# PEER decoder kernel: VectorE makes the low part of every second expert weight tile instead of every fourth

## The reference

```
h = rmsnorm(x) * (1 + sc1) + sh1;   x = x + g1 * mixer(h)      # RG-LRU heads and gated DeltaNet heads
h = rmsnorm(x) * (1 + sc2) + sh2;   x = x + g2 * peer(h)
y = rmsnorm(x)

peer: q = h @ peer_wq; scores of 8 heads x 2 halves against 128 keys; top 16 of each half,
      top 16 of their sums -> 16 experts idx (of 16384) and softmax gates for each head
      act = gelu(sum_d u[idx, d] * h[d]);  out = sum_k gates_k * act_k * v[idx_k]
```

## Time and profile before

| | us |
|---|---|
| median of 3 executions | 4352.23 (4347.91 to 4360.71) |
| the profiled execution | 4374.36 |
| its span in the trace | 4372.5 |
| TensorE matmul busy | 3735.8 (85%) |
| VectorE busy | 3022.4 (69%) |
| GpSimd busy | 2100.9 (48%) |
| ScalarE busy | 1476.1 (34%) |
| DMA moved | 1090.19 MB, mean 249 GB/s |

### The profile page before, as it was taken

One profiled execution on the slowest core, in us unless ns is written; L12 is line 12 of the kernel. 1 busy time (PEld: TensorE's weight loads), 2 busy tenths in 40 slices (PEclk: granted clock), 3 DMA queues, 4 the chain that ended last, 5 costly groups with the idle time before them and its releaser, 6 DMA issues. The chain is left out here.

```text
span 4372.5 us, 65820 instructions
## 1 busy us (share of the span) xinstructions
PE 3735.8 (85%) x24298; PEld 3475.5 (79%) x24298; DVE 3022.4 (69%) x4531; ACT 1476.1 (34%) x1889; POOL 2100.9 (48%) x1164
## 2 busy tenths in 40 slices
PE   6876999998896898987669999999988888888887
PEld 3336888988886797987569898889988888888886
DVE  5777645455545223898967777777878888888886
ACT  5665343434442113222323333333332222222222
POOL 2433222222224233324346777677766767666662
PEclk9997999999997998998889999999999999999898
DMA  8981222222222123223369999999999999999994
GB/s 308 355 319 51 83 79 83 73 79 71 68 69 97 54 96 110 82 71 106 144 269 389 414 406 405 393 402 409 399 376 378 394 387 402 388 400 399 408 403 154
DMA packets 253104, 1090.19 MB, mean 249 GB/s; under 512 B 25353, under 2 KB 78857, under 8 KB 172297
## 3 DMA queue, kind: packets, MB, share of 16 engines
q1 hardware_dynamic: 167440, 543.60, 33.8%
q0 software_dynamic: 73728, 536.90, 30.1%
q10 hardware_dynamic: 11776, 7.52, 0.6%
HBM read 1047.54 MB, written 40.40 MB: 249 GB/s over the span
## 5 line engine op out<-in xcount | busy, mean ns | idle before, releaser
L248 POOL TENSOR_TENSOR wlo<-raw,whi 128x1024 fp32r<-128x1024 f32 x551 | 1342.5, 2440 | 1470.8 <-ACT whi L244 1465.4
L244 ACT CAST whi<-raw 128x1024 fp32r<-128x1024 f32 x670 | 697.0, 1049 | 1242.0 <-DMA raw<-in_u 541.0
L263 PE MATMUL gps<-hi_d,whi 128*128 128x320 f32 x2048 | 663.1, 324 | 161.5 <-POOL wlo L248 108.0
L2110 PE MATMUL gps<-chi,whi 128*128 128x320 f32 x2048 | 651.1, 318 | 101.6 <-DVE outacc L2239 85.0
L263 PE MATMUL gps<-lo_d,whi 128*128 128x320 f32 x2048 | 653.6, 319 | 0.0
L263 PE MATMUL gps<-hi_d,wlo 128*128 128x320 f32 x2048 | 652.8, 319 | 0.0
L2110 PE MATMUL gps<-clo,whi 128*128 128x320 f32 x2048 | 640.7, 313 | 0.0
L2110 PE MATMUL gps<-chi,wlo 128*128 128x320 f32 x2048 | 640.6, 313 | 0.0
L2197 DVE SCALAR_TENSOR_TENSOR dps<-ring,coef,dps 128x2048 f32<-128x2048 f32 x252 | 591.6, 2348 | 6.3 <-DMA ring<-in_v_rows,spi 1.6
L2184 DVE CUSTOM_DVE_ANT_0 ring<-ring,dps 128x2048 f32<-128x2048 f32 x256 | 581.9, 2278 | 0.0
L263 PEld LDWEIGHTS gps<-hi_d,whi 128*128 128x128 f32 x2048 | 404.0, 197 | 179.0 <-POOL wlo L248 118.1
(11 more groups left out here) (388 smaller groups left out, 6026.6 us busy)
## 6 DMA issues: line engine op xcount, KB each, us to landing
raw<-in_u SPq DMA_DIRECT2D x256, 512.0 KB, 10.6
raw<-in_v SPq DMA_DIRECT2D x256, 512.0 KB, 7.8
wada<-in_w_ada SPq DMA_DIRECT2D x96, 1024.0 KB, 6.5
raw<-in_w_in SPq DMA_DIRECT2D x96, 512.0 KB, 3.5
gateD<-gst SPq DMA_DIRECT2D x8, 2560.0 KB, 7.5
gate<-gateD SPq DMA_DIRECT2D x32, 640.0 KB, 17.3
raw<-in_w_out SPq DMA_DIRECT2D x32, 512.0 KB, 3.6
raw<-in_w_q SPq DMA_DIRECT2D x32, 512.0 KB, 4.0
```

The costliest lines, as they stand in the source:

```text
L244: act.copy(whi[:, k.slot, :], raw_of(k)).then_inc(W.hi, 1)
L248: pool.tensor_tensor(wlo[:, k.slot, :], raw_of(k), whi[:, k.slot, :].bitcast(F32), ALU.subtract).then_inc(W.lo, 1)
L263: m = pe.matmul(gps[:, bank, 0:DT], w, x[:, kt, :], start=(kt == 0 and n == 0), stop=(kt == KT - 1 and n == 2))
L2110: m = pe.matmul(gps[:, 2 + dt, 0:DT], w[:, slot, cols], x[:, buf, c, :], start=(c == 0 and n == 0), stop=(c == NG - 1 and n == 2))
```

## The change

`by_dve` now picks the slots 1 and 3 from tile 181 on and no longer slot 3 alone from 183 on: VectorE makes tiles j = 1, 3, 5, 7 of each piece, GpSimd j = 0, 2, 4, 6. The counts in `lo_done` follow (two low parts of each engine in four tiles), and one more empty instruction raises the start value of VectorE's semaphore. The instructions themselves, the buffers and the order of each engine's list are the same; 124 low parts leave GpSimd's list and stand in VectorE's (123 before, 247 after), in A behind `clo` of step c, in B between the two additions of a step.

```diff
         def by_dve(k):
 
-            return k.c >= N_SHARED - 1 and k.slot == 3
+            return k.c >= N_SHARED - 3 and k.slot % 2 == 1 and not (isinstance(k.n, int) and k.n < N_SHARED)
 
         def lo_done(k):
 
             m = k.c - N_SHARED
             if by_dve(k):
-                return W.lo_dve, m // 4 + 2 + k.i * (k.per // 4)
+                return W.lo_dve, m // 2 + 3 + k.i * (k.per // 2)
             if m < -4 or m < 0 and isinstance(k.n, int):
                 return W.lo, k.n + 1
-            return W.lo, N_SHARED + m // 4 * 3 + m % 4 + 1 + k.i * (k.per // 4 * 3)
+            return W.lo, N_SHARED + m // 2 + 1 + k.i * (k.per // 2)
...
-                    dve.engine_nop().then_inc(W.lo_dve, 1)
+                    for n in range(2):
+                        dve.engine_nop().then_inc(W.lo_dve, 1)
```

## The result

The changed kernel takes 4480.33 us (median of 4, 4477.44 to 4483.45) against 4355.02 us before: a ratio of 1.0274, 95% interval 1.025 to 1.0298. That is 125 us more, where 52 us had been forecast, and above the range of 4322 to 4465 us. The direction was right, and so was the place in A as the source of the loss; what the prediction took off for slack was wrong.

A forecast was written before the change was run, and what follows sets the result against it. Three resources were taken as near their ends: TensorE, VectorE and the transfers, at 95% of 418 GB/s. 16 x 1.0 + 13 x 2.5 + 3 = 51.5 us more gave 4404 us on the median's scale, range 4322 to 4465 us.

The forecast's parts named there:

- the range: Whole kernel's time: from 4322 us (half of Rival 3) to 4465 us (short of rival 1's full price).
- the place in A: In A, low parts j = 3 and 7 come late for TensorE: 2.5 us a period (first stretch), 4.5 (second).
- GpSimd's relief gives nothing on the path: GpSimd loses 124 low parts, 299 us, but isn't the bound, so by itself this gives nothing.
- VectorE's load: VectorE gains 124 low parts; second stretch busy time goes from 58.8 to 66.1 us of a 71.0 us period.
- B: In B, VectorE's eight steps go to 29.0 us against TensorE's 28.1; bounds 0 and 1.0 us, 0.5 taken.
- The last B: In the last B, j = 3 and 7 could make TensorE wait 0 to 8.4 us; 3 taken.
- What is absorbed: Waits for late weights cover part of the raw 3.0 and 5.0 us a period; 1.0 and 2.5 us kept.
- rival 1: Nothing is absorbed in either stretch: 116 us more, 4468 us; chance 0.13.
- Rival 2: Transfers hide it all, periods stay 65.3 and 71.0 us, only the tail counts: 4355 us; chance 0.20.
- Rival 3: Faster: with GpSimd relieved, loads start sooner; 47 us less, 4305 us, or 4329 with half eaten; chance 0.23.
- The port: VectorE's second SBUF input shares GpSimd's interface: 35 us more VectorE load in the first stretch, left out of the sum.

The follow-up runs named there:

- b_only: Kernel before, but VectorE makes low parts j = 1, 3, 5, 7 in pieces B, still j = 1, 5 in pieces A: 4354.12 us, 0.9982.
- best: b_only with VectorE's low part in A right behind the gate multiplication, in the first stretch only: 4357.55 us, 0.9982.
- place_after: Changed kernel with VectorE's low part in A right behind the gate multiplication, no longer behind take and `clo`: 4400.91 us, 1.0081.
- place_before: Kernel before with VectorE's low part in A right behind the gate multiplication: 4366.41 us, 1.0006.
- a_only: Kernel before, but VectorE makes low parts j = 1, 3, 5, 7 in pieces A, still j = 1, 5 in pieces B: 4461.34 us, 1.0224.
- gate_small_before: Kernel before with gate loads of an eighth of the size (80 KB, not 640 KB), same place in SyncE's order: 4260.13 us, 0.9756.
- gate_small_after: Changed kernel with gate loads of an eighth of the size (80 KB, not 640 KB): 4406.53 us, 1.0097.
- a_j7: Kernel before with only tile j = 7 of the pieces A given to VectorE besides j = 1, 5 of every piece: 4400.77 us, 1.0086.
- early_j3: Changed kernel with only the low part of tile j = 3 of A right behind the gate multiplication (step c = 0): 4424.87 us, 1.0121.
- early_j7: Changed kernel with only the low part of tile j = 7 of A right behind the gate multiplication (step c = 2): 4426.47 us, 1.0136.

## Why the prediction was wrong, step by step

*GpSimd's relief gives nothing on the path*: right. Its busy time fell from 2100.9 to 1866.8 us, and the kernel got slower; b_only and best show no gain clear of the noise.

*VectorE's load*: 66.1 us a period forecast for the second stretch, 874.47 / 13 = 67.3 measured. The sum has no term for the larger share itself, only for its place and for B; place_after against place_before puts 34.5 us on it. The low parts there became longer than taken, 2032 ns on average against 1815, as more of them meet GpSimd's. With the early place they are 1458 ns (151.7 / 104).

*The place in A*: right in mechanism and nearly in size. Forecast about 30 and 35 waits, 8.6 and about 10 us from gate to gate; measured 31 and 38, 8.7 and 10.0 us. Forecast 2.5 us of waiting more in a period of the first stretch, measured 3.0. For the second 4.5, measured 5.0, and the step with j = 3 lost 1.7 us where 1.1 was taken. Summed over the three steps of A the second stretch lost 4.7 us a period.

*B*: forecast 0.5 us a period raw. b_only shows none and a_only to the whole change 0.4 and 0.7 us, so within the bounds of 0 and 1.0 us.

*The last B*: forecast 3 us, measured 1.1 us behind the last piece A. The last piece A itself, which the sum had not counted as one of 30, took 5.8 us.

*What is absorbed*: this is the step that failed, "I keep a third in the first stretch (1.0 us) and half in the second (2.5 us)": the prediction took two thirds and half of the raw price off. Measured was 3.4 us (4.3 in the first five periods) and 3.6 us: 58.9 us against 16 in the first stretch, 46.3 against 32.5 in the second. The 2.8 us of waits for late weights were taken for slack that a later TensorE would find filled. In the first stretch they were none for the two stops of this change: 28.5 of the 31.0 us stayed, and gate_small_before and gate_small_after lose 3.2 us a period without any late weights. Those weights are late by their place in SyncE's order, a place counted from TensorE's own progress. In the second stretch the cover was real (3.0 us), but it falls in the step with j = 3, which grows by 4.1 us where no weights are late and by 1.7 us where they are. The 1.1 us that the prediction had put on that step were already the price after this cover; half of the 5.0 us took it off a second time. What came back beyond it was the 1.1 us between two pieces A. So it was wrong to take a wait for weights as slack where nothing said that the transfers' rate made that wait; the DMA share of 1.00 hid that a stop of TensorE also stops the fetches, and 397 GB/s fell to 376.

*Rivals*: rival 1, nothing absorbed, named 116 us and 4468 us and had 0.13; measured 125 us, 103 in the traces. It was right in kind for the first stretch (3.0 us named, 3.4 measured); in the second it named 5.0 us and 3.6 were lost, so that its sum comes close is in part luck. Rival 2 fell with the periods of 68.4 and 74.6 us and the transfers at 376 and 378 GB/s. Rival 3's mechanism shows in b_only's second stretch alone, and its gain did not repeat in best.

*The range*: its lower end is called half of rival 3, which by the prediction's own sum is 4329 us and not 4322; nothing hangs on it.

*The port*: the Trainium skill's page VectorE: DVE Perf Modes, section Two Vector instructions with no wait between them, says that VectorE reads its second SBUF input through an interface shared with GpSimd. The trace agrees: VectorE's low parts in the second stretch took 2367 ns in the median and 1212 ns at the shortest. Its further use, 35 us more load in the first stretch, did not come: the mean there is 114.9 / 88 = 1.31 us.

**Left open.** In the first stretch a_j7 got back 1.1 us between two pieces A, and early_j3, which has the same stop and VectorE's larger share besides, did not. The traces overstate the gap: a_j7's is of its fastest execution and early_j3's of its slowest, 39 us apart where the ratios are 0.35 points (15 us) apart with intervals that overlap. Executions of the kernel before on one chip lay between 4349.90 and 4390.17 us, which is 1.4 us a period, so differences of 1 us between single traces settle nothing. What the larger share costs at the early place (34.5 us) has no cause shown either.

## What to carry to other kernels

A faster instruction is worth nothing, or costs, if it stands behind a long one in the list of the engine that is to run it: ask by when the consumer needs it and what is in front of it there, not how busy the two engines are. Count a wait as slack only after asking what sets the arrival that is waited for; if that is issued relative to the waiting engine's own progress, it moves along, and delays add up. Slack covers a first stop better than the next: in the second stretch one late tile beyond j = 5 cost 0.9 to 1.4 us a period (early_j7, early_j3, a_j7) and the next 1.5 to 2.7 us (to a_only and the changed kernel). So price stops in order and not with one factor, and ask whether the price of a stop already holds the cover.

## What the runs showed of the hardware

A subtraction of two fp32 tiles of 128 x 1024 in SBUF takes VectorE 1.22 us and GpSimd 2.41 us; where GpSimd's is already running VectorE's ends about 1.1 us after it and so takes up to 3.30 us in the changed kernel; where VectorE's began first it keeps 1.22 us and GpSimd's grows, at most to 3.42 us. VectorE's takes, with one input in PSUM, keep their 2.28 and 2.35 us beside it. The transfers of weights and rows together reached 410 to 412 GB/s over a whole stretch, once the 640 KB gate loads came in four parts between the weight loads; with them in one piece a tile behind took 14.8 us from issue to rounding, and the stretches ran at 394 to 397 GB/s.
